# Two merge-gate weight chunks beside the neighbourhood attention: two plain products, or one Strassen pair

## What is computed

```python
h = jnp.concatenate([h_ctx, h_lat], axis=1)
(na_q, na_k, na_v, na_gate, pool_u, pool_gate, rw_r, rw_k, rw_v, rw_gate,
 rw_lw, rw_la, merge_logits) = jnp.split(h @ w_in, IN_SPLIT_POINTS, axis=-1)
...
s = jnp.concatenate([s_loc.reshape(B, H, GRID_W, n_loc), s_ctx], axis=-1)
p = jax.nn.softmax(s, axis=-1).astype(v.dtype)
...
g_na, g_pool, g_rw = jnp.split(jax.nn.sigmoid(keep(merge_logits)), N_BRANCH, axis=-1)
merged = g_na * (b_na @ w_branch[0]) + g_pool * (b_pool @ w_branch[1]) + g_rw * (b_rw @ w_branch[2])
```

## Time and profile before

| | us |
|---|---|
| median of three runs | 3815.72 |
| lowest, highest run | 3815.25, 3823.80 |
| the profiled execution's own time | 3821.46 |
| span of the profiled execution | 3819.7 |
| the attention stage `att_h` in it | 2410.3 to 2562.0 |

### The profile page before, as it was taken

One profiled execution on the slowest core, in us unless ns is written; L12 is line 12 of the kernel. 1 busy time (PEld: TensorE's weight loads), 2 busy tenths in 40 slices (PEclk: granted clock), 3 DMA queues, 4 the chain that ended last, 5 costly groups with the idle time before them and its releaser, 6 DMA issues. The chain is left out here.

```text
span 3819.7 us, 60114 instructions
## 1 busy us (share of the span) xinstructions
PE 3569.4 (93%) x24813; PEld 1824.9 (48%) x24813; DVE 2045.4 (54%) x3262; ACT 686.9 (18%) x1375; POOL 560.4 (15%) x801
## 2 busy tenths in 40 slices
PE   8799998999989999899999999898998889899998
PEld 1354443434544446454444444453346666665443
DVE  0399994433337867456646657335533444334435
ACT  0100000121320112232100000235532222221000
POOL 0011111021000001100000011541212423322100
PEclk9999999999999999999999999999999999999999
DMA  8778996794245556526556586648863333335663
GB/s 293 286 278 308 351 368 236 284 340 159 72 150 188 187 195 217 186 82 227 203 200 250 208 317 229 221 141 289 269 212 119 115 123 105 106 107 175 233 229 110
DMA packets 362559, 799.05 MB, mean 209 GB/s; under 512 B 26574, under 2 KB 73702, under 8 KB 357674
## 3 DMA queue, kind: packets, MB, share of 16 engines
q1 hardware_dynamic: 259920, 459.69, 35.2%
q0 software_dynamic: 72736, 274.10, 20.0%
q10 hardware_dynamic: 29634, 61.45, 4.2%
HBM read 686.94 MB, written 108.22 MB: 208 GB/s over the span
## 5 line engine op out<-in xcount | busy, mean ns | idle before, releaser
L1444 PE MATMUL gemm_a_g_ps<-store_w,turned 128*128 128x512 f32 (+1 forms) x1152 | 456.8, 559 | 2.4 <-PEq L205 2.4
L975 DVE SCALAR_TENSOR_TENSOR pmods_acc<-pmods_w,cond,pmods_acc 128x512 f32<-128x512 f32 x540 | 384.3, 748 | 24.2 <-issue 1.3
L1444 PEld LDWEIGHTS gemm_a_g_ps<-store_w,turned 128*128 128x128 f32 x1152 | 209.0, 191 | 249.7 <-issue 249.7
L3300 PE MATMUL scan_g_ps<-store_w,turned 64*64 64x512 f32 x2048 | 285.6, 604 | 9.8 <-DVE outlet_stage L3314 6.9
L1444 PE MATMUL att_a_g_ps<-store_w,turned 128*128 128x512 f32 x512 | 240.2, 599 | 6.9 <-ACT outlet_stage L3028 4.2
L1444 PE MATMUL feat_g_ps<-store_w,turned 128*128 128x512 f32 x384 | 181.9, 623 | 14.6 <-ACT outlet_stage L2456 12.4
L1491 PE MATMUL out_c_g_ps<-store_w,turned 128*128 128x512 f32 x384 | 167.6, 592 | 0.0
L1444 PE MATMUL tail_g_ps<-store_w,tail_branch_t 128*128 128x512 f32 x384 | 165.7, 592 | 0.9 <-ACT tail_branch_t L4129 0.9
L3665 DVE TENSOR_TENSOR scan_tm<-scan_tm,scan_ps 128x256 f32<-128x256 f32 x128 | 53.8, 421 | 164.9 <-PE scan_ps L3553 164.7
L1444 PEld LDWEIGHTS att_a_g_ps<-store_w,turned 128*128 128x128 f32 x512 | 91.5, 191 | 100.1 <-issue 93.4
L3553 PE MATMUL scan_ps<-scan_tmt,scan_y 64*64 64x64 f32 x2560 | 118.4, 222 | 15.0 <-issue 11.7
(11 more groups left out here) (568 smaller groups left out, 5945.8 us busy)
## 6 DMA issues: line engine op xcount, KB each, us to landing
store_w<-in_w_in SPq DMA_DIRECT2D x160, 1024.0 KB, 7.8
pmods_w<-in_w_mod POOLq DMA_DIRECT2D x40, 2048.0 KB, 12.1
store_w<-in_a_w_in SPq DMA_DIRECT2D x48, 1024.0 KB, 11.3
store_w<-in_c_w_in SPq DMA_DIRECT2D x40, 1024.0 KB, 8.5
mods_w<-in_w_mod SPq DMA_DIRECT2D x32, 1024.0 KB, 9.3
store_w<-in_a_w_out SPq DMA_DIRECT2D x32, 1024.0 KB, 6.1
scan_raw<-s_feat SPq DMA_DIRECT2D x112, 256.0 KB, 4.7
s_feat<-feat_o POOLq DMA_DIRECT2D x16, 1536.0 KB, 7.5
```

Of the source, the lines that this page charges most:

```text
L975: v.scalar_tensor_tensor(a, src, x, a, ALU.mult, ALU.add)
L1444: mm = pe.matmul(to, lhs, self.store.slot[i % self.store.NS][:, k, :width], start=first, stop=last)
L3300: mm = pe.matmul(self.ps[r][halves[o], :], self.act_tile(k, tb)[halves[r], halves[o]], self.store.slot[i % self.store.NS][halves[r], k % 4 ...
```

## The change

The first two merge chunks are wrapped as one pair, and the stage gets `inputs=h_summed` in place of the plain view of `turned`:

```diff
-        merge_early, merge_late, merge_last = merge_chunks(0, 2), merge_chunks(2, 8) + merge_chunks(10, 12), in_pairs(merge_chunks(8, 10))
+        merge_early, merge_late, merge_last = in_pairs(merge_chunks(0, 2)), merge_chunks(2, 8) + merge_chunks(10, 12), in_pairs(merge_chunks(8, 10))
...
-        attend_and_project(nc, "att_h", store, outlet, ident, NeighbourhoodPlan(proj_h, mix_h[0], C, tiled), 1.0, 64, xt(512), merge_early,
-                           10, None)
+        attend_and_project(nc, "att_h", store, outlet, ident, NeighbourhoodPlan(proj_h, mix_h[0], C, tiled), 1.0, 64, None, merge_early,
+                           10, None, inputs=h_summed)
```

## The result

The pair is slower. Nine runs of the changed kernel have a median of 3831.03 us (3828.36 to 3838.65), nine of the kernel before 3819.49 us (3815.25 to 3823.80). The ratio is 1.0034, with a 95% interval from 1.0023 to 1.0044: 13 us, between 9 and 17 (the medians differ by 11.5). The forecast was 3821.9, with 3829 as its upper end and "same", up to 3827.2, as the likeliest class. The measured median lies above both. In size it is 0.34% where "same" was to end at 0.3%, and the interval holds both sides of that line. The direction was right: it is slower, not faster.

A forecast was written before the change was run, and what follows sets the result against it. The stage was taken as a chain through four engines, not bound by TensorE alone. -1.9 (matmuls) + 4.4 (sums) + 2.0 + 1.0 (start, clock) + 0.7 (end) = +6.2 us, so a median of 3821.9 us, range 3811 to 3829.

The forecast's parts named there:

- the loop's 2.5 us: Attention stage, score 0 to score 31: removed matmuls gain 1.9 us, sums on VectorE cost 4.4 us.
- The start: Stage start: an early weight load shares the queues, turn and masks 2.0 us later, plus 1.0 us for a clock fall.
- rival 1: Attention stage: TensorE is the bound after all, sums fit in the room; -6.9 + 0.7, so 3809.5 us; chance 0.12.
- A removed matmul: Attention steps: each of eight second matmuls is worth 0.70 us in a turning step, 0.09 us elsewhere; gain 1.9 us.
- A lone piece: Steps 2, 12, 15, 22: one weight sum ahead of the scaling delays reciprocal and next score by 0.26 us each.
- Step 17: Attention stage: a weight piece and result sum y01 ahead of the scaling cost 0.9 us.
- Step 20: Steps 18 to 20: a late maximum meets ScalarE's sigmoid table load for y01; 0.65 us passes on to TensorE.
- Rival 3: Steps 10, 14, 22: weight sums collide with GpSimd's masks and wait about 0.7 us; +1.5 us, 3823.4; chance 0.08.
- the heap's wait: Step 10: a piece, u2 and u4 ahead of one scaling cost 1.65 us, a gap of 2.4 us less the turn.
- Rival 2: Attention stage: opened gaps make the clock fall four times at 1.8 us each; +12.4 us, 3828.1; chance 0.10.
- The end: Stage end: the last product needs a VectorE sum before its activation, 0.7 us more.
- y00: Step 30: the result sum y00 stands alone, shorter than VectorE's room, and costs nothing.

The follow-up runs named there:

- the experiment on the kernel before: Kernel before, with the second projection matmul of its four turning steps moved one step later, none removed: loop 128.86 us, ratio 1.0006.
- thin pieces: Changed kernel with this stage's weight sums of forms 2, 3 and 4 made for 1 column in place of 512: loop 126.64 us, ratio 1.0003.
- the best placement: Changed kernel, sums behind the scaling only in steps without a turn, u2 and u4 apart, turning steps' second matmuls one step later: loop 124.79 us, ratio 1.0003.

## Why the prediction was wrong, point by point

In short: the loop's 2.5 us left out two things that the prediction had named and priced as rivals, the pieces' wait for the masks (measured 1.8 us) and a clock fall (1.6 us), and one that it had not, VectorE's stops. And its base was 3.8 us too low. The start's 3.0 us were 2.5 too many and hid part of it.

- **What bounds the stage: right.** Removing work from TensorE made it wait more. A stage shorter than 151 us would have made rival 1 right; it is longer.
- **A removed matmul: right.** 0.66 and 0.65 in turning steps against 0.70, 0.04 to 0.11 elsewhere against 0.09; the experiment on the kernel before confirms both to 0.05.
- **A lone piece: right where nothing else runs.** Step 12 took 4.27 (about 4.25 forecast). Step 17, piece and y01, 0.83 against 0.81. Step 20 was sized 0.65 and measured 0.96.
- **The step that failed first: "Rival 3", given 0.08.** The prediction said a piece would wait for the end of a mask, and gave a lone 1.5 us. Its size was nearly right (about 0.7 of waiting for each place, measured 0.5), its chance was not. Masks run in steps 2, 6, 10, 14, 18, 22 and 25; pieces stand beside them in four (2, 10, 14, 22), and the prediction saw three. Measured: 0.52 + 0.54 + 0.53 in steps 2, 10 and 22 and 0.2 behind step 14 = 1.8 us. The rows of step 22 fit a wait of each for the other: 0.61 + 1.15 for the piece, the piece's end + 1.11 for the second addition. The rule of the Trainium skill, "SBUF — State Buffer", section "SBUF: two separate sides", that such a pair takes the shared ports in turn and the second blocks, agrees with them. With the masks all but gone the piece was back at 1.23.
- **The second: the heap's wait and the clock, "Rival 2", given 0.10.** The wait was forecast as 2.4 us less the turn, and was 2.25, since the three sums took some 0.5 more beside the masks (with the masks out it was 1.72). Behind it stood a fall of 1.6 us in four of four profiles, and none in the one profile each of the versions that made this wait shorter. The rival had up to four falls of 1.8. There was mostly one.
- **The third: two stops of 0.43 us**, steps 4 and 15, a term that the prediction didn't have. Step 4 is 0.43 over its forecast, and with thin pieces, or pieces behind the scaling, its stop cost nothing (4.08, 4.07). Step 15 is 0.42 over, of which 0.2 went with the masks. 0.65 us for both, by these sizes; no run took a stop out. The kernel before has a stop of this size in its loop as well, in step 29, which took 3.99 us as others do:

```profile
2544.52 0.15 DVE L2920 TENSOR_SCALAR att_h_stat<-att_h_stat 128x1 f32<-128x1 f32 x1 [0.43 <-issue]
```

- **The start: over-sized.** 2.0 us and 1.0 for a clock fall became 0.5 for the turn and 0.4 in step 1, without a fall. The prediction had q0 at 0.17 MB in every microsecond from 2419 on, so 0.75 MB in 4.4 us. It got 0.27, 0.23 and 0.23 MB in the first three, 0.73 in all, and the masks' 0.9 us fit that. I took the share of q0 from a microsecond in which it got 0.17 MB in 66 packets beside 90 of q1. From 2420 to 2421 it had 66 packets as q1 had, but of 3.5 KB each, against 2.0 KB in q1. Equal packets are not equal bytes. This is argued from the rows of the queues; no run tested it. The rule of the Trainium skill, "DMA: Bandwidth & Descriptors", section "Queues, rings and completion order", speaks of turns by packet. 66 beside 66 agrees; 66 beside 90, which the prediction took for agreement, doesn't, so the rows bear the rule out only in part. That I made equal bytes of it was my step, not the page's.
- **The end: right**, 0.7.
- **The sum.** Forecast 2.5 + 3.0 + 0.7 = 6.2; measured 8.2 + 0.5 + 0.7 = 9.4, in four profiles 9.8. The loop's 5.7 too little: fall 1.7, collision 1.8, stops 0.65, first masks 0.4, table load 0.3, step 27 0.2, and some 0.6 in rests, mostly 0.04 in each step whose own score had waited. Around step 27 ScalarE loads its tables (2541.66 and 2544.61) for y00, which the prediction had at nothing; the kernel before has such loads around steps 12 and 15, which took 4.11 and 4.16. No run tested that. The start's 2.5 too much hid half of it.
- **The base.** I moved the sum from the profiled 3821.46 to the median of three runs, 3815.72. The median of 9 runs was 3819.49, and of 29, 35 and 17 later ones 3821.35, 3819.51 and 3820.47. So of the 9.1 us between 3821.9 and 3831.03, 3.8 are the base, and 5.3 the change. From 3819.49 the same working would have given 3825.7 and an upper end of 3832.8: the time fell out of the range by the base, while the change itself was forecast at about half of its 11.5 us.

## What to carry to other kernels

Work moved to an idle engine is cheap by where it stands in that engine's list, not by the idle share: ahead of the instruction that the busy engine waits for, each sum costs its length less the room; behind it, and in a step that does nothing else there, it costs nothing (placing the sums and two matmuls elsewhere, without one less, took the loop from 134.4 to 124.8, 1.6 of it the clock fall). The same holds for the work that is taken away: a matmul was worth 0.65 us where it stood in the busy engine's way and 0.1 where it filled a wait, so it counts which steps lose one, not how many are gone. Lay the lists of all engines side by side before pricing, since a sum beside GpSimd's masks, two sums ahead of one scaling, or a table load without cover are read there. And a median of three runs that differ by 8 us is no base for a forecast of 6 us.

## What the runs showed that I had not expected

- The clock's fall isn't set by the length of the last wait: 2.25 us had one in four of four profiles, 2.69 us (in another version) none, 1.42 and 1.59 us in one of four, and one came behind waits of 0.7 us. With all 64 matmuls and the second ones moved, two came, behind 1.52 and 0.84 us. Each cost 1.6 us in this loop.
- A VectorE sum of 128x1024 and GpSimd's two additions of 128x512 hardly overlap: 1.22 and 2.50 us apart, 3.72 in sum; 1.76 and 3.48 side by side, with all three done 3.48 us after the first began. The sum u2, which reads PSUM for one input, kept its 0.68 inside that.
- VectorE stood 0.43 us with nothing to wait for in steps 4 and 15, in every profile of the pair but that of the best placement, which has only the first. The kernel before has neither, but one of the same size in step 29, and others long before the stage (at 234.38, 356.31 and 590.13 us, 0.43 to 0.45 us each). So they aren't peculiar to the pair; what the pair did was to put its pieces where two of them count. The cause is open.
- In the kernel before, step 5 hangs on GpSimd issuing four-buffered stores behind its loads: 0, 0.3 or 0.6 us in three profiles, 0.8 and a clock fall when the matmuls came earlier.
